# Products with few output rows, put into four 32-column strips of the matrix engine

## The reference, cut to what matters

```python
sc, scc = silu(c), silu(c_ctx)                    # two conditioning vectors of 1024
mod_p = scc @ w_mod[l] + b_mod[l]                 # 1024 -> 3072, in every layer
mod_s = sc  @ w_mod[l] + b_mod[l]
shift, scale, gate = split(mod, 3)
h = rmsnorm(x, g) * (1 + scale) + shift           # then x = x + gate * mixer(h)

# mLSTM: 16 gate rows (2 kinds x 2 directions x 4 heads) from q, k, v of 2048 each
ipre = einsum('btc,dch->dbht', concat(q, k, v), w_ig) + b_ig
lf   = log_sigmoid(einsum('btc,dch->dbht', concat(q, k, v), w_fg) + b_fg)

# GLA: the decay is a product of rank 16, for each of two directions
la = log_sigmoid((h @ w_a1[d]) @ w_a2[d] + b_a[d]) / 16
```

## Time and profile before

| | |
|---|---|
| executions | 1946.92, 1950.22, 1950.91 us |
| span of the profiled execution | 1948.8 us, 16614 instructions |
| TensorE busy | 1816.9 us (93%) |
| VectorE, ScalarE, GpSimd busy | 604.2 (31%), 495.2 (25%), 167.7 us (9%) |
| mean granted TensorE clock | 0.968 of 2.4 GHz |
| DMA | 185.98 MB, 95 GB/s over the span |

### The profile page before, as it was taken

The page is one execution under the profiler, slowest core; times in us unless marked ns, Lnnn a source line. Parts: engine busy times, 40 slices in busy tenths (PEclk is TensorE's granted clock), DMA queues, the critical chain, the costliest instruction groups (busy, mean ns, idle before and its releaser), DMA issues.

```text
span 1948.8 us, 16614 instructions
## 1 busy us (share of the span) xinstructions
PE 1816.9 (93%) x6421; PEld 1050.9 (54%) x6421; DVE 604.2 (31%) x979; ACT 495.2 (25%) x960; POOL 167.7 (9%) x158
## 2 busy tenths in 40 slices
PE   6899999999989899988989998999799998898998
PEld 3355534755655554546455455545455536575655
DVE  0333005336340202375320552321433005445420
ACT  2201323323320114343111222231201223433300
POOL 1000001001000000052043000000100001100100
PEclk9999998999999998999999997999899999999999
DMA  6522222233242321242365221323222221212122
GB/s 189 203 86 86 88 74 76 76 112 116 83 146 95 113 86 43 76 150 98 130 126 156 86 86 44 98 98 110 73 86 87 99 74 44 83 48 87 44 88 75
DMA packets 105140, 185.98 MB, mean 95 GB/s; under 512 B 5136, under 2 KB 54704, under 8 KB 105072
## 3 DMA queue, kind: packets, MB, share of 16 engines
q1 hardware_dynamic: 95816, 158.40, 24.2%
q0 software_dynamic: 8640, 26.46, 4.6%
q10 hardware_dynamic: 616, 0.16, 0.1%
HBM read 164.47 MB, written 20.54 MB: 95 GB/s over the span
## 4 chain that ended last, share of the span: by engine, by line
PE 88%; DVE 5%; ACT 3%; issue 1%; DMA 1%; SPq 0%; DVEq 0%; ACTq 0%; POOLq 0%
PE acc L500 69%; PE mix L500 17%; PE acc L565 1%; DMA out_new_C<-cst 1%; DVE hT L1523 1%; ACT cp L1276 1%; DVE mix L1344 1%; DVE rd L1505 1%; DVE cstat L1666 1%; PE mix L915 0%; DMA ring<-in_a_w_out 0%; DMA cst<-in_c_k_g 0%; DVE dx L1590 0%; DVE hT L1348 0%; DVE fqk L1626 0%
## 5 line engine op out<-in xcount | busy, mean ns | idle before, releaser
L500 PE MATMUL acc<-hT,ring 128*128 128x385 f32 x1664 | 548.3, 491 | 15.8 <-DVE hT L1351 14.4
L500 PEld LDWEIGHTS acc<-hT,ring 128*128 128x128 f32 x1664 | 317.9, 192 | 244.6 <-issue 21.9
L500 PE MATMUL acc<-z,ring 128*128 128x385 f32 x512 | 169.5, 492 | 6.1 <-DMA ring<-in_a_w_out 4.2
L500 PE MATMUL acc<-ring,sc 128*2 128x384 f32 x512 | 170.2, 486 | 1.6 <-ACT mst L992 1.2
L500 PEld LDWEIGHTS acc<-z,ring 128*128 128x128 f32 x512 | 97.9, 192 | 77.7 <-issue 6.1
L500 PE MATMUL mix<-qs,ring 128*128 128x256 f32 x512 | 117.6, 392 | 9.6 <-DVE qs L1507 9.6
L500 PEld LDWEIGHTS mix<-qs,ring 128*128 128x128 f32 x512 | 100.1, 197 | 27.6 <-issue 13.2
L500 PEld LDWEIGHTS acc<-ring,sc 128*2 128x2 f32 x512 | 41.3, 85 | 119.1 <-issue 112.2
L1363 DVE SCALAR_TENSOR_TENSOR y<-acc,modv,y 128x128 f32 x64 | 23.4, 413 | 223.8 <-PE acc L500 223.8
L500 PE MATMUL acc<-ring,hT 128*128 128x512 f32 x192 | 85.5, 608 | 0.0
L500 PE MATMUL acc<-xc,bd 128*128 128x385 f32 x128 | 57.5, 574 | 14.2 <-DVE hT L1523 8.4
(11 more groups left out here) (297 smaller groups left out, 2212.6 us busy)
## 6 DMA issues: line engine op xcount, KB each, us to landing
ring<-in_w_mod SPq DMA_DIRECT2D x64, 768.0 KB, 6.2
ring<-in_a_w_in SPq DMA_DIRECT2D x32, 1024.0 KB, 6.9
ring<-in_state_mlstm_C SPq DMA_DIRECT2D x16, 1024.0 KB, 7.8
out_new_C<-cst POOLq DMA_DIRECT2D x32, 512.0 KB, 3.2
ring<-in_a_w_out SPq DMA_DIRECT2D x16, 1024.0 KB, 7.8
ring<-in_c_w_in SPq DMA_DIRECT2D x16, 1024.0 KB, 7.6
ring<-in_b_w_in SPq DMA_DIRECT2D x12, 1024.0 KB, 6.3
ring<-in_b_w_out SPq DMA_DIRECT2D x4, 1024.0 KB, 6.2
```

Of the source, the lines that this page charges most:

```text
L500: return nc.tensor.matmul(out, lhsT=lhsT, rhs=rhs, start=start, stop=stop)
```

## The change

The products with 2 or 16 rows of output run as matmuls with 32 weight columns whose outputs go in turn to PSUM rows 0 to 31, 32 to 63, 64 to 95 and 96 to 127, which makes the four 32-column strips of the array. Each strip sums a quarter of the blocks; the products that come after it add the four partial sums.

- Modulation: weights are 32 columns of `sc` (the block's two, then those of later blocks, zeros at the end). ScalarE copies 128 rows, and the three transposes become matmuls with a selector `sel`, whose two columns hold a 1 in rows 0, 32, 64, 96 and in 1, 33, 65, 97.
- Gate: 32 columns of `gfold` (16 wanted, 16 that the selector leaves out); `gfold` moves to the buffer `aq`, and `gsel` gets four copies of its selecting block.
- Decay: 32 columns of `ga1`, and `ga2` is loaded four times, once into each strip's rows, with zeros between.

```diff
+            def quarters(ps, count, lhsT, rhs):
+                for n in range(count):
+                    j = n % 4
+                    ins = mm(ps[32 * j:32 * j + 32, :], lhsT(n), rhs(n), n < 4, n >= count - 4)
+                return ins
...
             def mod_columns(l, n):
-                t = tile(f"modrow{n}", l)
-                moved(pe, t)
-                transposes(tile(f"modcol{n}", l), [
-                    (lambda ps, e=e: ps[:, 2 * e:2 * e + 2], mst[:, seg(n % 2 * MC + e * P, P)])
-                    for e in range(MC // P)])
+                moved(pe, tile(f"modrow{n}", l))
+                t = tile(f"modcol{n}", l)
+                ps = bank(t)
+                for e in range(MC // P):
+                    ins = mm(ps[:, 2 * e:2 * e + 2], mst[:, seg(n % 2 * MC + e * P, P)], sel[:, :], True, True)
+                ins.then_inc(acc_ready, 1)
...
-                group(ps[0:2, 0:MC], [(sc[:, 2 * k:2 * k + 2], w3[:, k, :]) for k in range(KD)]
-                      ).then_inc(acc_ready, 1)
+                quarters(ps[:, 0:MC], KD, lambda k: sc[:, 2 * k:2 * k + 32], lambda k: w3[:, k, :]
+                         ).then_inc(acc_ready, 1)
...
-                for n, (a, b) in enumerate(pairs):
+                def gate_input(n):
                     if n == AT_:
                         pe.wait_ge(xc_ready, AT_ * (ia + 1))
-                    ins = mm(ps[0:16, 0:W], a, b, n == 0, n == len(pairs) - 1)
-                ins.then_inc(acc_ready, 1)
+                    return xm3[:, n, 1:1 + W] if n < AT_ else xc3[:, n - AT_, :]
+                quarters(ps[:, 0:W], 2 * AT_, lambda n: gfold[:, seg((2 * (n % AT_) + (n < AT_)) * 16, 32)], gate_input
+                         ).then_inc(acc_ready, 1)
...
-                pe.wait_ge(b_in, 16 * 5)
+                pe.wait_ge(b_in, 16 * 11)
                 for d in range(2):
-                    group(bank(tile("la", l, d))[0:RANK, 0:W], [(ga14[:, k, d, :], h3[:, k, :]) for k in range(KD)]
-                          ).then_inc(acc_ready, 1)
+                    quarters(bank(tile("la", l, d))[:, 0:W], KD, lambda k: ga1[:, seg((2 * k + d) * RANK, 32)],
+                             lambda k: h3[:, k, :]).then_inc(acc_ready, 1)
...
             moved(pe, tile("vec", 0, 1))
+            pe.wait_ge(sel_ready, 1)
...
-                move(tile(f"modrow{n}", l), mst[:, seg(n % 2 * MC, MC)], lambda ps: ps[0:2, 0:MC])
+                move(tile(f"modrow{n}", l), mst[:, seg(n % 2 * MC, MC)], lambda ps: ps[:, 0:MC])
...
+                if l == 0:
+                    nc.vector.tensor_reduce(sel, ident.rearrange("p (j r) -> p r j", r=32)[:, 0:2, :], AX, ALU.add
+                                            ).then_inc(sel_ready, 1)
...
-                nc.vector.tensor_copy(gsel.rearrange("p (n c) -> p n c", c=32)[:, :, 0:AH],
-                                      ident[0:16, 0:16].rearrange("p (n c) -> p n c", c=AH)).then_inc(gsel_ready, 1)
+                for q in range(4):
+                    r = seg(32 * q, 16)
+                    ins = nc.vector.tensor_copy(gsel[r, :].rearrange("p (n c) -> p n c", c=32)[:, :, 0:AH],
+                                                ident[r, r].rearrange("p (n c) -> p n c", c=AH))
+                ins.then_inc(gsel_ready, 1)
...
+                nc.gpsimd.memset(ga1[:, KD * 2 * RANK:KD * 2 * RANK + 16], 0.0)
+                link(nc.gpsimd.memset(ga2, 0.0))
...
-                    pool.dma_start(ga2[:, seg(d * BH * BDK, BH * BDK)], i["b_w_a2"][0, d]).then_inc(b_in, 16)
+                    for q in range(4):
+                        pool.dma_start(ga2[seg(32 * q, RANK), seg(d * BH * BDK, BH * BDK)], i["b_w_a2"][0, d]
+                                       ).then_inc(b_in, 16)
```

More of the change, by code:

```diff
@@ L138, in trunk @@
         vec = sb("vec", 4 * P)
-        sc = sb("sc", 2 * KD)
+        sc = sb("sc", 2 * KD + 32)
+        sel = sb("sel", 2)
         modv = sb("modv", 3 * KD * 2)
         modr = sb("modr", 3 * KD * 2)
-        mst = sb("mst", 2 * MC, rows=2)
+        mst = sb("mst", 2 * MC)
         rstd = sb("rstd", W)
@@ L191, in trunk @@
         nst = r_ab[0:2, 0:ADH]
-        gfold = kw[0]
-        grow = kw[1][0:16, 0:TC]
-        gsel = kw[1][0:16, TC:TC + P]
+        gfold = aq[:, 0:ADH + 16]
+        grow = kw[1][:, 0:TC]
+        gsel = kw[1][:, TC:TC + P]
         vrow = cst[0][:, 0:4 * P]
@@ L204, in trunk @@
         bd4 = bd.rearrange("p (m e c) -> p m e c", m=3, e=HT)
-        g4 = gfold.rearrange("p (f s n) -> p f s n", s=2, n=16)
+        g4 = gfold[:, 0:ADH].rearrange("p (f s n) -> p f s n", s=2, n=16)
         qs3 = [v3(t, HT, NLAT) for t in qs]
@@ L229, in trunk @@
             gmask = sb("gmask", LEVELS * P, I32, stack=st)
-            ga1 = sb("ga1", KD * 2 * RANK, stack=st)
-            ga2 = sb("ga2", 2 * BH * BDK, rows=RANK, stack=st)
-            gha = sb("gha", 2 * W, rows=RANK, stack=st)
+            ga1 = sb("ga1", KD * 2 * RANK + 16, stack=st)
+            ga2 = sb("ga2", 2 * BH * BDK, stack=st)
+            gha = sb("gha", 2 * W, stack=st)
         gq3, gk3, gv3, gr3 = v3(gq, BH, TC), v3(gk, BH, TC), v3(gv, NT, D), v3(gr, KD)
         gb4 = gb.rearrange("p (d h t) -> p d h t", d=2, h=BH)
-        ga14 = ga1.rearrange("p (k d n) -> p k d n", k=KD, d=2)
+        ga14 = ga1[:, 0:KD * 2 * RANK].rearrange("p (k d n) -> p k d n", k=KD, d=2)
         gs03, kft3 = v3(gs0, 2 * BH, BDV), v3(kft, 2 * BH, P)
@@ L276, in trunk @@
         gsel_ready = sem("gsel_ready")
+        sel_ready = sem("sel_ready")
         sq_ready = sem("sq_ready")
@@ L759, in mlstm @@
                 pe.wait_ge(gfold_ready, ia + 1)
-                pairs = [(g4[:, f, 1, :], xm3[:, f, 1:1 + W]) for f in range(AT_)]
-                pairs += [(g4[:, f, 0, :], xc3[:, f, :]) for f in range(AT_)]
                 ps = bank(t)
-                for n, (a, b) in enumerate(pairs):
+                def gate_input(n):
                     if n == AT_:
                         pe.wait_ge(xc_ready, AT_ * (ia + 1))
-                    ins = mm(ps[0:16, 0:W], a, b, n == 0, n == len(pairs) - 1)
-                ins.then_inc(acc_ready, 1)
+                    return xm3[:, n, 1:1 + W] if n < AT_ else xc3[:, n - AT_, :]
+                quarters(ps[:, 0:W], 2 * AT_, lambda n: gfold[:, seg((2 * (n % AT_) + (n < AT_)) * 16, 32)], gate_input
+                         ).then_inc(acc_ready, 1)
                 moved(pe, t)
@@ L1018, in _ @@
             move(tile("vec", 0, 0), vec[:, :])
-            move(tile("vec", 0, 1), sc.rearrange("p (k r) -> p r k", r=2),
+            move(tile("vec", 0, 1), sc[:, 0:2 * KD].rearrange("p (k r) -> p r k", r=2),
                  lambda ps: ps[:, V_CTX - 2 * P:V_CTX - 2 * P + 16].rearrange("p (r k) -> p r k", r=2), ACT.Silu)
@@ L1137, in mlstm @@
                 ps = ready(tile("gate", l, 0))
-                nc.scalar.copy(grow[:, 0:P], ps[0:16, 0:P])
-                move(tile("gate", l, 0), grow[:, P:TC], lambda ps: ps[0:16, LAT:W])
+                nc.scalar.copy(grow[:, 0:P], ps[:, 0:P])
+                move(tile("gate", l, 0), grow[:, P:TC], lambda ps: ps[:, LAT:W])
                 move(tile("gate", l, 1), r_ig, lambda ps: ps[0:64, 0:TC], ACT.Identity, bias=rowp[:, ia:ia + 1])
@@ L1178, in gla @@
                 for d in range(2):
-                    move(tile("la", l, d), gha[:, d * W:(d + 1) * W], lambda ps: ps[0:RANK, 0:W])
+                    move(tile("la", l, d), gha[:, d * W:(d + 1) * W], lambda ps: ps[:, 0:W])
                 for n in range(2 * BH):
@@ L1322, in _ @@
             for t, x in ((vrow[:, :], 0.0), (rowp[:, :], 0.0), (eps[:, :], EPS), (ones[:, :], 1.0),
-                         (ones_d[:, :], 1.0 / D), (ones_h[:, :], 1.0 / ADH),
+                         (ones_d[:, :], 1.0 / D), (ones_h[:, :], 1.0 / ADH), (sc[:, :], 0.0),
                          (y3[:, :, NCTX:LAT], 0.0)):
@@ L1378, in prepare @@
                 done_before(dve, l - 1)
-                for t in (xm3[:, :, 0:1], xm3[:, :, W + 1:W + 2], gsel, r_ab[:, :], r_m[:, :]):
+                for t in (xm3[:, :, 0:1], xm3[:, :, W + 1:W + 2], gsel, gfold[:, ADH:ADH + 16], r_ab[:, :], r_m[:, :]):
                     ins = nc.vector.memset(t, 0.0)
```

## The result

The changed kernel takes 1827.09 us (median of four executions, 1826.1 to 1830.04) against 1949.3 for the kernel before on the same chip: ratio 0.9381, 95% interval 0.9367 to 0.9395. It is the time of the prediction's first rival (1834).

The account below looks back on a forecast made before the run. TensorE was taken as the bound (busy 1816.9 of 1948.8 us). Savings of 13.0 + 14.0 + 2.0 + 3.5 + 14.0 + 19.4 + 4.3 - 0.5 = 69.7 gave 1948.8 - 69.7 + 1.4 = 1880.5, say 1880; range 1830 to 1928.

Parts of the forecast that it names:

- rival 1: Strip matmuls: all four strips run at once, a group saves 3.87 - 0.15 us; 116 us in all, 1834; chance 0.14.
- the price of a group: Modulation group of 8 matmuls: nine passes of 0.322 us, 2.90 us, instead of 16; 2.15 us saved after weight loads.
- The decay and the v product: Decay's first product, two groups: 4.3 us saved in the forecast, 7.5 in rival 1; the v product behind was left out.
- the clock's 4 us: Behind the decay's 16-row passes PE's clock was 0.50 for 10.3 us; full rows might save some 4, left out.
- Heads: Layer 0's heads, 8 modulation parts: 14.0 us saved in the forecast, 24 in rival 1, where VectorE's products end late.
- GLA's two terms: GLA levels (6 parts) and GLA end (2 parts): 2.0 and 3.5 us saved in the forecast, 3 and 6.6 in rival 1.
- The selector: Three transposes of a modulation part become six passes of 0.65 to 0.8 us; 0.4 us more per part.
- GLA levels: Six parts between levels: 2.0 of 10.5 us saved, because PE already waits for VectorE and GpSimd, which hold each other up.
- The margins in heads and attention: Layer 0's heads and attention layer: shorter parts still cover VectorE's chain to qs and the softmax chain; 14.0 us saved each.
- rival 3: Heads, attention and GLA: VectorE and ScalarE set the pace, parts were only cover; 36 us left, 1914; chance 0.12.
- rival 2: Strip matmuls: no overlap, only costs stay, 11 us slower, 1961, or 1984 with strip changes priced; chance 0.18.
- Refills: Start of layer 0: slot refills take 6.7 us; the forecast charged 1.0 for the stage, rival 1 1.3 six times.

Follow-up runs that it names:

- one_strip: The changed kernel, but every 32-column matmul goes to strip 0 instead of four strips in turn: 1959.39 us, 1.0046 of the kernel before.

## Why the prediction was wrong in size

**The step that failed** is the price of a group: "the two passes of one matmul use one strip and stand next to each other, so the second waits for the first; the matmul after it can start beside that second pass". The first half is so, the second is not. The second pass waits in its strip, and the next matmul starts beside its first, in its own (four starts within the 60 ns shown above). A group is four rounds of 0.322 us, not nine: 1.42 us to the next start against 5.25 before, 3.83 saved where 2.15 were forecast. With that one number the forecast's own method is rival 1, 1834. Its chance of 0.14 was too low: the argument against it, program order, had no row behind it.

**Mis-sized terms.** Rival 1's 116 us against some 122 measured. The decay and the v product gave 12.0 instead of 7.5: the clock's 4 us that the prediction named and left out; with them in rival 1's sum the foot of the range would have been near 1826 instead of 1830 and held the time. Heads: 26.4 for 24; VectorE's products end late in the first head alone, a wait of 0.21 us. GLA's two terms gave 7.0 instead of rival 1's 9.6: at GLA's end TensorE now waits 1.10 us for ScalarE between the two parts (0.30 before) and 1.65 us for the weights of the output product. So the nearness of 116 to 122 is in part luck: the clock's share and GLA's shortfall offset each other. One reading of the start was off without effect: part 2 has a length of 5.43 us in the earlier trace rows, where the prediction added 5.32, the length of the other parts.

**Right.** The selector: 0.69 us, in the 0.65 to 0.8 given. GLA levels: 2.7 for 2.0, by the reason given. The margins in heads and attention, which rival 3 doubted: no wait for `qs` in layer 0, and the scores wait 0.56 us for the exponentials as before. No overlap, rival 2: `one_strip` is 1959.4 for 1961, though rival 2 left out both the clock behind the decay, which gives some 4 us back, and the 2 to 4 us by which the selector cost more than 11. Refills: rival 1 charged 1.3 us six times, 7.8, and 7.2 us of waits appeared, in four of the parts. The weight loads do lie under running matmuls of the same rows. That the gate's second half would not wait for `xc` holds as well: its group has no idle time.

## What to carry to other kernels

A matmul with few weight columns leaves most of the array idle: put independent partial sums into its four column strips, in turn, and, as far as these runs go, not more than four passes in a row in one. Price such work where TensorE sets the end: saved passes between products that VectorE sets were worth a seventh of their length here, and a shortened stage uncovered its transfers. When a cost is bounded from both sides and nothing in the trace says where it lies, let the range reach the end, with the side effects that go with it.

## What the runs showed that was not expected

- A strip takes one running and three waiting passes before it holds up the others (17.1 us for a gate of 16 in a row, 5.4 in turn).
- Eight loads of 32 weight columns are under way within 60 ns, and four passes at once that share all 128 rows and stream 384 columns each follow one another in their strips every 0.32 us, as one alone does.
- 112 zero rows kept the granted clock at 1.00 where 16-row passes were followed by 0.50, and the kernel with them was 2 to 6 us faster.
- Three transposes of whole 128 x 128 blocks take 0.39 us, six passes with 2 moving columns 0.69.
